# The ring of weight buffers starts 32 bytes further on in the on-chip memory

## What is computed

```
for l in range(2):                                  # first block
    proj  = h @ w_in[l]
    mixed = concat(nsa(...), gla(...), pool(...))   # three mixers on slices of proj
    h = layer_norm(ALPHA * h + mixed @ w_out[l])
    ff = square(relu(h @ w_up[l])) @ w_down[l]
    h = layer_norm(ALPHA * h + ff)
for i in range(2):                                  # second block
    h = h + 0.5 * rms_norm(swiglu(rms_norm(h), wi, wo))
    h = h + rms_norm((dilated, window)[i](rms_norm(h)))
    h = h + 0.5 * rms_norm(swiglu(rms_norm(h), wi, wo))
    h = h + rms_norm((p[i] @ ple_proj) * sigmoid(rms_norm(h) @ ple_gate))
```

## Time and profile before

| | value |
|---|---|
| median of three runs | 3295.49 us |
| lowest and highest | 3287.92 and 3302.30 us |
| the profiled execution, device time | 3295.67 us |
| its span, first to last instruction | 3293.5 us |
| TensorE busy | 3241.8 us (98%), 16,870 matmuls |
| VectorE / ScalarE / GpSimd busy | 55% / 38% / 10% |
| share of TensorE in the chain that ended last | 89% |

### The profile page before, as it was taken

The page is one execution under the profiler, slowest core; times in us unless marked ns, Lnnn a source line. Parts: engine busy times, 40 slices in busy tenths (PEclk is TensorE's granted clock), DMA queues, the critical chain, the costliest instruction groups (busy, mean ns, idle before and its releaser), DMA issues.

```text
span 3293.5 us, 43153 instructions
## 1 busy us (share of the span) xinstructions
PE 3241.8 (98%) x16870; PEld 2642.0 (80%) x16870; DVE 1818.4 (55%) x2946; ACT 1240.1 (38%) x1882; POOL 332.1 (10%) x242
## 2 busy tenths in 40 slices
PE   8999999999999999999999999999999999999999
PEld 7768888776788888888788778888888886788887
DVE  6776334677752446443666664435644367654436
ACT  3355232425542324332333343324433235533325
POOL 0300000231100020000223100000000012000001
PEclk9999999999999999999999999999999999999999
DMA  4112232321132232223322222332232321133332
GB/s 169 65 46 77 96 102 97 132 73 46 46 107 98 96 103 83 98 99 109 111 71 71 69 84 97 102 108 97 90 102 96 109 99 46 59 102 102 102 109 83
DMA packets 81433, 300.39 MB, mean 91 GB/s; under 512 B 9040, under 2 KB 9040, under 8 KB 80640
## 3 DMA queue, kind: packets, MB, share of 16 engines
q1 hardware_dynamic: 78624, 284.20, 25.9%
q0 software_dynamic: 1568, 11.98, 0.9%
q10 hardware_dynamic: 1088, 2.10, 0.2%
HBM read 296.14 MB, written 2.10 MB: 91 GB/s over the span
## 4 chain that ended last, share of the span: by engine, by line
PE 89%; DVE 5%; ACT 3%; issue 2%; POOL 1%; DMA 1%; POOLq 0%; ACTq 0%; DVEq 0%
PE bank L920 25%; PE bank L922 25%; PE bank L921 25%; PE bank L964 2%; PE bank L971 2%; PE bank L965 2%; ACT sc L1824 1%; PE bank L1248 1%; DVE wl L2153 1%; PE bank L1489 1%; PE bank L1501 1%; PE bank L1229 1%; PE bank L1544 1%; ACT wh L1652 1%; PE bank L1263 1%
## 5 line engine op out<-in xcount | busy, mean ns | idle before, releaser
L920 PE MATMUL bank<-x,wh 128*128 128x512 f32 x2616 | 1023.0, 391 | 4.7 <-DVE wl L2153 2.9
L922 PE MATMUL bank<-x,wl 128*128 128x512 f32 x2616 | 999.4, 382 | 0.0
L921 PE MATMUL bank<-x,wh 128*128 128x512 f32 x2616 | 999.0, 382 | 0.0
L2153 DVE TENSOR_TENSOR wl<-raw,wh 128x1024 fp32r<-128x1024 f32 x526 | 669.7, 1274 | 518.2 <-ACT wh L1652 516.9
L1652 ACT ACTIVATE wh<-raw 128x1024 fp32r<-128x1024 f32 x526 | 554.4, 1054 | 1065.5 <-PE bank L922 1013.8
L920 PEld LDWEIGHTS bank<-x,wh 128*128 128x128 f32 x2616 | 490.9, 188 | 111.9 <-issue 23.0
L922 PEld LDWEIGHTS bank<-x,wl 128*128 128x128 f32 x2616 | 490.6, 188 | 88.9
L921 PEld LDWEIGHTS bank<-x,wh 128*128 128x128 f32 x2616 | 491.4, 188 | 85.6 <-issue 3.8
L920 PE MATMUL bank<-mid,wh 128*128 128x512 f32 x1216 | 465.5, 383 | 1.2 <-DVE wl L2153 1.2
L922 PE MATMUL bank<-mid,wl 128*128 128x512 f32 x1216 | 463.7, 381 | 0.0
L921 PE MATMUL bank<-mid,wh 128*128 128x512 f32 x1216 | 463.7, 381 | 0.0
(11 more groups left out here) (377 smaller groups left out, 3314.4 us busy)
## 6 DMA issues: line engine op xcount, KB each, us to landing
raw<-stream SPq DMA_DIRECT2D x526, 512.0 KB, 3.3
raw_apart<-stream SPq DMA_DIRECT2D x12, 512.0 KB, 3.7
sm<-small POOLq DMA_DIRECT2D x2, 2144.0 KB, 10.5
tb<-tab POOLq DMA_DIRECT2D x2, 1728.0 KB, 14.8
h<-x_t ACTq DMA_DIRECT2D x4, 512.0 KB, 6.8
out_t<-h SPq DMA_DIRECT2D x8, 256.0 KB, 2.7
tba<-tab_a POOLq DMA_DIRECT2D x1, 1152.0 KB, 7.7
pf<-p_t POOLq DMA_DIRECT2D x2, 512.0 KB, 6.0
```

The source lines that it names most:

```text
L920: pe.matmul(dst, hi, xh, start=start, stop=False)
L921: pe.matmul(dst, hi, xl, start=False, stop=False)
L922: return pe.matmul(dst, lo, xh, start=False, stop=stop)
L2153: dve.tensor_tensor(low_of(n)[:, :], raw_of(n)[:, :], high_of(n)[:, :].bitcast(F32), ALU.subtract).then_inc(split_done, 1)
```

## The change

The gap between `y` and the ring grows from 192 to 224 bytes:

```diff
         px = at("px", [P, 2, 2, S], F32R, offset=x_at + 6 * 2 * S * 4)
-        place[0] += 192
+        place[0] += 224
         raw = [at(f"raw{i}", [P, UNIT]) for i in range(4)]
```

## The result

The changed kernel takes 3323.47 us (median of six runs, 3308.20 to 3330.67) against 3294.06 us before (six runs, 3287.92 to 3302.30). The ratio is 1.0082, with a 95% interval of 1.0066 to 1.0098: slower by 0.82%, which is some 27 us (the two medians lie 29 us apart). The profiled execution of the changed kernel took 3308.2 us, which is the fastest of its six; its span is 3306.1 us, 12.6 us over the 3293.5 us of before. The other five runs took 3322.69 to 3330.67 us.

A forecast was written before the change was run, and what follows sets the result against it. TensorE, 98% busy, was taken to bound the kernel through the pace of its dense matmul stream. All terms were taken as zero, so 3295.67 us plus 0 gave about 3296 us, with a range of 3268 to 3340 us.

The forecast's parts named there:

- likeliest case: Whole kernel: four second-block stretches stay at 220 ns, others among 220 to 224; 3280 to 3312 us, chance 0.42.
- the prediction's own sign: Six long dense stretches: the prediction is wrong if the second block's four leave 220 ns (1456 or 1457 matmuls in 320 us).
- The lever: Dense matmul stream: 1 ns of pace over 12,912 matmuls is worth 12.9 us, 0.39% of the time.
- The terms taken as zero: Splits on ScalarE and VectorE, other moved buffers' evictions and norms, raw-unit transfers: each zero; ranges include transfers 0 to +5.6 us.
- its bound of +12: Splits on ScalarE and VectorE: address effect taken as zero, bounded at -32 to +12 ns per split.
- such a small shift is mostly taken up by the stream's own settling: Dense stream: the 32-byte shift leaves the four stretches at 220 ns and the others among 220 to 224; sum zero.
- Two of the 16-byte pieces: Dense stream: 32 bytes called two 16-byte pieces of the activations' reading and a sixteenth of a weight tile, a small shift.
- The slow rival: Second block's four long stretches lose 220 ns: 3315 us at 223.2 ns, 3346 us at 228.3; chance 0.37.
- its own 6000 matmuls: Second block's four long stretches: about 1500 matmuls each, 6000 together, used to price a slower pace.
- the fast rival: First block (-7.7 us) and remaining matmuls, mixers included (at most 12.9 us), find 220 ns too: 3275 us; chance 0.13.
- The rhythm below 220: Dense stream: a rhythm of 218 ns may exist; with all 12,912 matmuls in it 3249 us; chance 0.08.
- The rule on the read ports: TensorE: independent read ports would make the weights' address worth nothing, sum zero; not used as reason, lowers no rival's chance.

The follow-up runs named there:

- the eight gaps: Kernel before with the ring's gap at 192 (before), 224 (changed), 704, 448, 0, 96, 64 or 160 bytes; ratios to before from 0.9999 (704) to 1.0280 (160).
- plain order: Kernel before (gap 192) with dense-matmul columns read and written in plain order, not four passes of 16 bytes every 64; ratio 1.0275 (1.0251 to 1.0299).

## Why the prediction was right or wrong

The time, 3323 us, lies inside the range of 3268 to 3340 us, but not where the prediction put its likeliest case: 3296 us and "same" with 0.42. What came is the rival to which it gave 0.37. So the range holds the time because it made room for that rival, and not because the reasoning behind the forecast was right; in that the hit is luck. By the prediction's own sign it was wrong: three of the four stretches left 220.

**The lever was right.** The prediction read out of the windows and the timeline that only the pace of the dense stream can answer to an address, at 12.9 us per ns. In the table above the pace accounts for all but 5 us of the 105 between the spans.

**The terms taken as zero were right.** ScalarE's split went from 1057 to 1060 ns, within its bound of +12; VectorE's stayed at 1225, the landing at 3.3 us, the waits for low parts at 9.6 us against 11.1. Moving the buffers behind the ring, also taken as zero, was wrong in effect though not in its reason: their operations take no longer, but moving them alone costs 0.35% through the choice of rhythm in the stretches behind. The prediction had bounded their own durations only.

**The step that failed** is "such a small shift is mostly taken up by the stream's own settling". It took the rhythms as belonging to the stream and the distance as a starting point within them. The runs show the reverse: each distance has a set of its own, in the profiles {220, 222.7, 223.4, 228.3} at 192, {220, 225.3} at 224, {231.7} at 160, and the start only picks within the set. "Two of the 16-byte pieces" was no small part of a period of 256 bytes, and 32 bytes to the other side cost 2.8%. The prediction could not see the period, since all its rows had only the distances 0 and 192; but its own reading, 386 against 380 ns in the earlier trace rows, had two distances with two behaviours, and should have weighed more. A run at distance 0 bears that row out: its stretches lie 3.4 and 6.7 ns above 220.

**The slow rival** named the right place, the four long stretches losing 220, and the size in the right frame: 19 us at 223.2, 50 us at 228.3. At the 225.3 that came, its own 6000 matmuls give 32 us. Its mechanism was only half right: it had the stretches fall into one of the rhythms of the old distance (222.7, 223.2 or 228.3), while 225.3 is a rhythm that no profile with the distance 192 has. Whether the unit that stands apart at the start of a stage has a part in it, no run tests. The median is 29 us slower; in the profiled run one of the four stayed and the first block gained, as the fast rival said of it (-7.8 us against the 7.7 it gave; the mixers did not follow, since the rest gained 4.2 us and not 12.9). So parts of two rivals happened at once in that run, and its +12.6 us would alone have passed for "same". Its argument that "a new placement can only keep that or lose it" held in all the gaps tried.

**The rhythm below 220** did not appear at any of the eight gaps or with plain order. Single matmuls of 378 or 379 ns, and single steps of 218 ns, are parts of mixed rhythms whose mean is 220 or more. The 216 ns that the prediction quotes are, in the section "Back-to-back issue gap" of the Trainium skill, "TensorE: Matmul & The Clock Gate", the gap of an isolated matmul. They were thus no floor for a stream with a weight load beside each matmul, where the lowest pace of a long stretch is 220.0 ns in all traces.

**The rule on the read ports.** The changed kernel and the gap of 160 have the instructions of the kernel before with the ring, and the buffers behind it, at another place, and their matmuls run at 225.3 and 231.7 against 220 ns; the ring alone brings the 225.3. The Trainium skill, "SBUF — State Buffer", section "Who interferes with whom", has it that TensorE's two read ports are independent and that TensorE waits on no one. The loads take as long in every trace (187 or 188 ns in the middle), and the pace is the same while no other engine works and no transfer runs (225.3 ns). What is left is that it matters for TensorE where its two streams read, so in its strict form the rule doesn't hold here for a 512-column fp32r matmul beside a weight load. That the two reads meet in the memory is the likely reading of this, but it is argued from the distance; what inside the memory makes the period of 256 bytes, no run here shows.

## What to carry to other kernels

Where a stream of matmuls with a weight load each bounds the time, measure the distance from start to start, not the busy share: a share of 98% to 99% busy hid paces from 220 to 231.7 ns, 5% of the pace. The distance of the weight buffers from the activations, by 256 bytes here, is then a size to be scanned like any other, in full, since neighbours 32 bytes apart were the best and the worst of those tried. A pace that differs between stretches of the same code on the same buffers is the sign of it, and one profile of such a kernel is one draw among several: compare medians.

## What the runs showed of the hardware that I had not expected

- The pace of 512-column fp32r matmuls depends on the distance of weights and moving operand, with a period of 256 bytes as far as tried: 220 to 228.3 ns at 192, 220 or 225.3 at 224, 231.7 at 160, 226.7 or 231.6 at 64, 226.2 at 96, 223.4 or 226.7 at 0. A common shift of all addresses by 32 bytes changes nothing that can be told (ratio 1.0007, 0.9993 to 1.0021). The other engines aren't needed for it: the pace at 224 is 225.3 ns also in the steps during which none of them works and no transfer runs.
- Some distances have several steady rhythms, each kept over some 1300 to 1500 matmuls, and executions of one kernel then differ by whole steps (3308 to 3331 us for the changed kernel); at the gap of 96 the profile shows one, and four runs agree within 0.6 us.
- No placement went below a mean of 220 ns in a long stretch at the full clock of 2.4 GHz (granted clock 1.00 in all windows).
